# MLP up-projections in a two-layer fp32 transformer: high and low activations side by side, streamed as one run of 512 columns

## The chip, the core and the metric

The kernel runs on one core of a Trainium2 chip. The metric is the device time of one execution in microseconds (us). Of the kernel before, three runs took 1045.91, 1046.89 and 1048.28 us, so the median is 1046.89 us.

## The reference, cut to what matters

Two blocks of a transformer are computed in fp32 for 256 tokens and a model width of 1024. The first block holds two mixing layers; the second holds two layers, each with a mixer, a cross attention and an MLP. Only the MLP is touched:

```
def sq_relu_mlp(h, w_in, w_out):
    return jnp.square(jax.nn.relu(h @ w_in)) @ w_out
```

`h` is 256 x 1024 (normalised tokens), `w_in` 1024 x 4096, `w_out` 4096 x 1024. It runs twice, once in each layer of the second block.

## The kernel before, in words

**Three products for one.** TensorE multiplies operands of the type fp32r, which holds fewer bits than fp32. So every fp32 operand is split into a high part (rounded to fp32r) and a low part (the rest), and a product is made of three matmuls into the same accumulator: high x high, high x low, low x high. The helper `three` (lines 471 to 477) issues them. In a matmul the first operand is the stationary one (128x128, loaded by a weight load of its own, LDWEIGHTS), the second one streams past it, one column after another. In the up-projections the weights are stationary and the activations stream: the names `w_hi`, `w_lo` are the weights' parts, `xT_hi`, `xT_lo` those of the transposed activations, each 128 x 8 chunks x 256 tokens. In the down-projections the activations `hT_hi`, `hT_lo` are stationary, and 512 columns of weights stream.

**Weights.** They arrive in units of 1 MB (2048 columns on 128 partitions) in five slots. SP issues the load of unit u when unit u - 5 has been used by TensorE (the semaphore `units_used`). ScalarE (ACT) then casts the unit's two halves to `w_hi` (line 1233), VectorE (DVE) subtracts to get `w_lo` (line 1715), and TensorE takes a unit when both are there (`lo_ready`).

**The MLP.** Its 4096 hidden features are worked off in 8 blocks of 512. A block needs two units for the up-projection (`up`, each covers 4 of the 8 chunks of the model width) and two for the down-projection (`down`). TensorE's order is written out by hand: first halves of up 0 and up 1, second halves of both, down 0, then for block 2 to 7 `up(blk)` followed by `down(blk - 1)`, and at the end down 7. The down-projections accumulate in banks 0 to 3 over all blocks. The up-projections use two pairs of banks by turns, 4 and 5 for even blocks, 6 and 7 for odd ones: one bank holds two groups of 128 features, 256 token columns each.

**From bank to next operand.** For each block and each of its two banks (pieces p of 128x512), ACT computes the relu out of the bank into `arena` (line 1628) and raises `relu_ready`; DVE squares it (line 2236, `h_ready`); ACT casts the square to `hT_hi` (line 1631, `hhi_ready`); DVE subtracts to get `hT_lo` (line 2239, `hT_ready`). `up(blk)` waits until both relus of block blk - 2 are done, `down(blk)` until both pieces of `hT_lo` are there. In ACT's and DVE's own queues, the work of a block (`step`) stands behind the casts and subtractions of the units up to those of the next up-projection (`splits(u + 6)`), and ahead of the two after them.

The instructions of one `up_half` before (one unit, 48 matmuls) come from these lines:

```
for f in range(4):
    o = banks[A_ + f // 2][:, (f % 2) * S:(f % 2 + 1) * S]
    for c in range(4):
        a = [flat(w, u)[:, c * BLK + f * P:c * BLK + (f + 1) * P] for w in (w_hi, w_lo)]
        ins = three(o, a, [v[:, 4 * n + c, :] for v in X], u, ...)
```

Of the kernel before, what the change touches and what calls it, by code (L numbers as in the profile page):

```python
# [21 lines left out]
ALU = mybir.AluOpType  # L22
# [3 lines left out]
F32R = mybir.dt.float32r  # L26
I32 = mybir.dt.int32

P = 128
D = 1024  # L30
S = 256
T = S // P
KC = D // P
# [10 lines left out]
DFF = 4 * D  # L44
BLK = 512
NBLK = DFF // BLK
MLA_QL, MLA_KVL, NOPE, ROPE, MLA_V = 384, 256, 128, 64, 128
LAM_INIT = 0.8 - 0.6 * math.exp(-0.3)
TWO_PI_HI = 6.28125
# [137 lines left out]
def build(nc, A, out):  # L187
    names, units = weight_units(A)
# [6 lines left out]
    with ExitStack() as ctx:  # L195
        def sb(name, shape, dt=F32):
            return ctx.enter_context(nc.sbuf_tensor(name, shape, dt))

        def sem(name):
            return ctx.enter_context(nc.semaphore(name))  # L200

        w_hi = sb("w_hi", [P, SLOTS, UNIT], F32R)
        raw_at = (nc.sbuf_base + 31) // 32 * 32
        raw = sb("raw", [P, SLOTS, UNIT])
        w_lo = nc.alloc_sbuf_tensor_at("w_lo", [P, SLOTS, UNIT], F32R, offset=raw_at)
        xT_hi = sb("xT_hi", [P, KC, S], F32R)
        xT_lo = sb("xT_lo", [P, KC, S], F32R)
        hT_hi = sb("hT_hi", [P, KC, S], F32R)
        hT_lo = sb("hT_lo", [P, KC, S], F32R)
        x = sb("x", [P, T, D])  # L210
# [24 lines left out]
        banks = [ctx.enter_context(nc.psum_tensor(f"bank{b}", [P, PANEL], F32)) for b in range(8)]  # L235
# [13 lines left out]
        units_used = sem("units_used")  # L249
        written = [sem(f"written{b}") for b in range(8)]  # L250
# [18 lines left out]
        fox_gate, fox_log, fox_sums, fox_ready = sem("fox_gate"), sem("fox_log"), sem("fox_sums"), sem("fox_ready")  # L269
        sb_log, sb_w, angle_ready, sine_ready, lam_sum, lam_exp, gains_ready = (sem(n) for n in ("sb_log", "sb_w", "angle_ready", "sine_ready", "lam_sum", "lam_exp", "gains_ready"))  # L270
        relu_ready, h_ready, hhi_ready, hT_ready = (sem(n) for n in ("relu_ready", "h_ready", "hhi_ready", "hT_ready"))
        setup_ready, out_ready, out_done = sem("setup_ready"), sem("out_ready"), sem("out_done")
        gained_ready, final_rstd, out_right_ready = sem("gained_ready"), sem("final_rstd"), sem("out_right_ready")

# [125 lines left out]
        mlp_base = {}  # L400
        released = {}

        def flat(buf, u):
            return buf[:, u % SLOTS, :]
# [34 lines left out]
        def _(pe):  # L439
            uses = [0] * 8  # L440
            freed = [None] * 8
# [489 lines left out]
            for c in range(5):  # L931
                o = banks[4][:, 0:S] if c < 3 else banks[4][:, S:2 * S]
# [86 lines left out]
            def mlp(i):  # L1019
# [2 lines left out]
                hb = [hT_blocks(v) for v in H]  # L1022

                base = {}
                relu0, hT0 = 2 * NBLK * i, 2 * NBLK * i

                def up_half(odd, n, u):

                    A_ = 4 + 2 * odd
                    take(u)  # L1030
# [4 lines that stand above are left out]
                            ins = three(o, a, [v[:, 4 * n + c, :] for v in X], u, n == 0 and f % 2 == 0 and c == 0, n == 1 and c == 3)  # L1035
                        if n == 1 and f == 1:
                            ins.then_inc(written[A_], 1)
                    ins.then_inc(units_used, 1)

                def up(odd, u, blk):  # L1040
                    pe.wait_ge(relu_ready, relu0 + 2 * (blk - 2) + 2)
                    for n in range(2):
                        up_half(odd, n, u + n)

                def down(odd, u, blk, first, last):

# [55 lines left out]
                down(0, u0 + 4, 0, True, False)  # L1102
                for blk in range(2, NBLK):
                    u = u0 + 6 + 4 * (blk - 2)
                    up(blk % 2, u, blk)
                    down(1 - blk % 2, u + 2, blk - 1, False, False)
                for b in (4, 6):
                    uses[b] += NBLK // 2
                for b in (4, 5, 6, 7):
                    freed[b] = [(relu_ready, relu0 + 2 * NBLK)]  # L1110
# [112 lines left out]
        def _(act):  # L1223
# [389 lines left out]
            def mlp(i):  # L1613
                x_turned(("p", i), U[("xo", i, 1), 0], U["mlp", i])
                u0 = names["mlp", i]
                h0 = 2 * NBLK * i

                def step(blk, u):

                    odd = blk % 2  # L1620
                    splits(u + 6 if blk else u + 5)
                    for p in range(2):
                        b = 4 + 2 * odd + p
                        if p == 0:
                            act.wait_ge(written[b], mlp_base[i][b] + blk // 2 + 1)
                        else:
                            act.wait_ge(units_used, max(u + 2, u0 + 3))
                        nc.scalar.activation(pan(4, p), banks[b][:, :], ACT.Relu).then_inc(relu_ready, 1)
                    for p in range(2):
                        act.wait_ge(h_ready, h0 + 2 * blk + p + 1)  # L1630
                        nc.scalar.copy(hb[:, 2 * odd + p, :], pan(5, p)).then_inc(hhi_ready, 1)

                used(u0 - 1)
                step(0, u0)
                step(1, u0 + 2)
                splits(u0 + 10)
                for blk in range(2, NBLK):
# [67 lines left out]
        def _(dve):  # L1705
# [518 lines left out]

            def mlp(i):
                x_turned(("p", i), ("xo", i), U[("xo", i, 1), 0], U["mlp", i])
                u0, h0 = names["mlp", i], 2 * NBLK * i

                def step(blk, u):
                    odd = blk % 2  # L2230
                    splits(u + 6 if blk else u + 5)
                    for p in range(2):
                        dve.wait_ge(relu_ready, h0 + 2 * blk + p + 1)
                        if p == 0 and (blk > 0 or i > 0):
                            dve.wait_ge(hT_ready, h0 + 2 * blk)
                        V.tensor_tensor(pan(5, p), pan(4, p), pan(4, p), ALU.mult).then_inc(h_ready, 1)
                    for p in range(2):
                        dve.wait_ge(hhi_ready, h0 + 2 * blk + p + 1)
                        V.tensor_tensor(hb[1][:, 2 * odd + p, :], pan(5, p), hb[0][:, 2 * odd + p, :].bitcast(F32),
                                        ALU.subtract).then_inc(hT_ready, 1)  # L2240

                used(u0 - 1)
                step(0, u0)
                step(1, u0 + 2)
                splits(u0 + 10)
                for blk in range(2, NBLK):
                    u = u0 + 6 + 4 * (blk - 2)
                    step(blk, u)
                    splits(u + 8)
# [207 lines left out]
```

## Time and profile before

| what | value |
|---|---|
| median of three runs | 1046.89 us |
| the profiled execution's own time | 1048.91 us |
| its span in the profile | 1047.1 us |
| PE busy, share of the span | 999.7 us, 95% |
| DVE / ACT busy | 629.9 us / 547.5 us |
| TensorE clock granted, mean over the span | 0.977 |
| first MLP, down 0 to the end of up 7 | 524.18 to 658.70 us |
| second MLP, the same stretch | 883.82 to 1018.34 us |

The times in the profile are of one execution: its span is 1047.1 us, and 1.81 us lie around it. A matmul's row in the timeline shows a start and a duration; matmuls are pipelined, so a row lasts longer than the distance to the next one. What one matmul costs a busy TensorE is therefore the distance from start to start, or the length of a stretch divided by its count.

### The profile page before, as it was taken

What the parts mean: (1) busy time and instruction counts of PE and PEld (TensorE: products, weight loads), DVE (VectorE), ACT (ScalarE), POOL (GpSimd) and SP (SyncE); (2) the same over time, 40 slices, a digit from 0 to 9 for tenths busy, and PEclk for the clock granted to TensorE, in tenths of its full rate; (3) what the DMA queues carried; (4) which work ended last, traced back from release to release, by engine and by line L of the source; (5) the groups of instructions that cost most, each with busy time, mean ns of one, the idle gap of its engine ahead of it and who ended that gap; (6) DMA issues with size and microseconds to landing.
All of it is one profiled execution on the core that took longest, in us unless ns stands there. A gap on an engine that the chain in (4) does not pass through costs nothing.

```text
span 1047.1 us, 15752 instructions
## 1 busy us (share of the span) xinstructions
PE 999.7 (95%) x6172; PEld 885.2 (85%) x6172; DVE 629.9 (60%) x1216; ACT 547.5 (52%) x1029; POOL 36.1 (3%) x83
## 2 busy tenths in 40 slices
PE   8999999998899979997999999999999899999997
PEld 7878788886787979895999999899988779999995
DVE  5877554676664476645765554557873658554554
ACT  6586553656474445534654444455663556444452
POOL 4021000001020000000000000000000000000000
PEclk9999989999899989999999999999999989999999
DMA  9975304454232434342555555656435425655651
GB/s 287 242 166 123 102 23 158 161 173 149 81 112 61 110 97 147 121 145 82 177 177 186 200 184 180 240 161 179 144 121 173 150 72 170 200 175 189 199 184 41
DMA packets 114166, 158.14 MB, mean 151 GB/s; under 512 B 13782, under 2 KB 55084, under 8 KB 114092
## 3 DMA queue, kind: packets, MB, share of 16 engines
q1 hardware_dynamic: 113656, 156.56, 48.3%
q8 instruction: 50, 0.82, 0.3%
q10 hardware_dynamic: 436, 0.56, 0.2%
q14 instruction: 24, 0.20, 0.1%
HBM read 156.06 MB, written 1.05 MB: 150 GB/s over the span
## 4 chain that ended last, share of the span: by engine, by line
PE 87%; DVE 7%; ACT 3%; issue 2%; DMA 0%; SPq 0%; DVEq 0%; ACTq 0%
PE bank L475 25%; PE bank L476 25%; PE bank L477 25%; DVE w_lo L1715 2%; PE bank L613 2%; PE bank L638 2%; PE bank L529 2%; PE bank L627 2%; PE bank L607 1%; ACT pb L1397 1%; ACT w_hi L1233 1%; PE bank L592 1%; PE bank L647 0%; DMA raw<-in_w_in_ab 0%; DVE arena L1925 0%
## 5 line engine op out<-in xcount | busy, mean ns | idle before, releaser
L1715 DVE TENSOR_TENSOR w_lo<-raw,w_hi 128x1024 fp32r<-128x1024 f32 (+2 forms) x292 | 335.9, 1196 | 189.6 <-ACT w_hi L1233 189.4
L1233 ACT CAST w_hi<-raw 128x1024 fp32r<-128x1024 f32 (+2 forms) x292 | 283.1, 1026 | 145.6 <-DMA raw<-in_mlp_w_in 76.0
L475 PE MATMUL bank<-xT_hi,w_hi 128*128 128x256 f32 x784 | 223.5, 285 | 2.7 <-DVE xT_lo L1772 1.8
L477 PE MATMUL bank<-xT_hi,w_lo 128*128 128x256 f32 x784 | 221.8, 283 | 0.0
L476 PE MATMUL bank<-xT_lo,w_hi 128*128 128x256 f32 x784 | 221.8, 283 | 0.0
L475 PE MATMUL bank<-w_hi,xT_hi 128*128 128x512 f32 (+1 forms) x432 | 162.7, 377 | 6.9 <-issue 3.2
L477 PE MATMUL bank<-w_hi,xT_lo 128*128 128x512 f32 (+1 forms) x432 | 158.7, 367 | 0.0
L476 PE MATMUL bank<-w_lo,xT_hi 128*128 128x512 f32 (+1 forms) x432 | 158.5, 367 | 0.0
L475 PEld LDWEIGHTS bank<-xT_hi,w_hi 128*128 128x128 f32 x784 | 150.3, 192 | 4.4 <-issue 2.6
L476 PEld LDWEIGHTS bank<-xT_lo,w_hi 128*128 128x128 f32 x784 | 150.3, 192 | 0.6
L477 PEld LDWEIGHTS bank<-xT_hi,w_lo 128*128 128x128 f32 x784 | 150.3, 192 | 0.0
L475 PE MATMUL bank<-w_hi,hT_hi 128*128 128x512 f32 (+2 forms) x384 | 143.8, 375 | 0.5 <-DVE hT_lo L1770 0.5
L476 PE MATMUL bank<-w_lo,hT_hi 128*128 128x512 f32 (+2 forms) x384 | 143.1, 373 | 0.0
L477 PE MATMUL bank<-w_hi,hT_lo 128*128 128x512 f32 (+2 forms) x384 | 142.7, 372 | 0.0
L475 PEld LDWEIGHTS bank<-w_hi,xT_hi 128*128 128x128 f32 x432 | 83.6, 194 | 20.9 <-issue 8.8
L477 PEld LDWEIGHTS bank<-w_hi,xT_lo 128*128 128x128 f32 x432 | 83.1, 192 | 13.4
L476 PEld LDWEIGHTS bank<-w_lo,xT_hi 128*128 128x128 f32 x432 | 83.6, 193 | 11.8
L475 PEld LDWEIGHTS bank<-w_hi,hT_hi 128*128 128x128 f32 x384 | 72.9, 190 | 13.3 <-DVE hT_lo L1770 0.9
L477 PEld LDWEIGHTS bank<-w_hi,hT_lo 128*128 128x128 f32 x384 | 72.6, 189 | 12.8
L476 PEld LDWEIGHTS bank<-w_lo,hT_hi 128*128 128x128 f32 x384 | 72.7, 189 | 11.9
L1772 DVE SCALAR_TENSOR_TENSOR xT_lo<-bank,gains,xT_hi 128x256 fp32r<-128x256 f32 x76 | 31.9, 478 | 37.8 <-ACT xT_hi L1278 37.8
L1291 ACT ACTIVATE xn<-x 128x512 f32<-128x512 f32 x32 | 20.1, 629 | 55.0 <-DVE x L1841 49.5
(242 smaller groups left out, 1107.7 us busy)
## 6 DMA issues: line engine op xcount, KB each, us to landing
raw<-in_mlp_w_in SPq DMA_DIRECT2D x32, 1024.0 KB, 5.3
raw<-in_mlp_w_out SPq DMA_DIRECT2D x32, 1024.0 KB, 5.1
raw<-in_w_in_ab SPq DMA_DIRECT2D x13, 1024.0 KB, 10.2
raw<-in_w_in_cd SPq DMA_DIRECT2D x13, 1024.0 KB, 5.2
raw<-in_xa_w_kv SPq DMA_DIRECT2D x8, 1024.0 KB, 5.2
raw<-in_sb_w_qkv SPq DMA_DIRECT2D x16, 512.0 KB, 5.1
raw<-in_w_out_ab SPq DMA_DIRECT2D x4, 1024.0 KB, 5.0
raw<-in_w_out_cd SPq DMA_DIRECT2D x4, 1024.0 KB, 5.1
```

The lines of the kernel that those rows point to most:

```text
L475: pe.matmul(o, wh, ih, start=start, stop=False, skip_group_check=True)
L476: pe.matmul(o, wh, il, start=False, stop=False, skip_group_check=True)
L477: return pe.matmul(o, wl, ih, start=False, stop=stop, skip_group_check=True)
L529: ins = pe.transpose(o, src(t, c), ident[:, :])
L592: ins = pe.transpose(o, arena[:, panel, t * w + c * P:t * w + (c + 1) * P], ident[:, :])
L613: ins = pe.matmul(banks[b][:, a:z], q(t * P, (t + 1) * P), kk(0, keys), start=n == 0, stop=n == len(k["parts"]) - 1)
L627: ins = pe.transpose(banks[6][:, n * P:(n + 1) * P], src[:, a:a + P], ident[:, :])
L638: ins = pe.matmul(banks[7][:, t * vd:(t + 1) * vd], k["pt"][:, n * P:(n + 1) * P], k["v"](kt), start=m == 0, stop=m == len(mine) - 1)
L1233: nc.scalar.copy(w_hi[:, u % SLOTS, a], raw[:, u % SLOTS, a]).then_inc(hi_ready, 1)
L1291: ins = nc.scalar.activation(xn[:, t, a], x[:, t, a], ACT.Square, accum_out=(guess if half else ssq)[:, c:c + 1])
L1715: V.tensor_tensor(w_lo[:, u % SLOTS, a], raw[:, u % SLOTS, a], w_hi[:, u % SLOTS, a].bitcast(F32), ALU.subtract).then_inc(lo_ready, 1)
L1772: ins = V.scalar_tensor_tensor(out=o, in0=ps, scalar=g, in1=hi.bitcast(F32), op0=ALU.mult, op1=ALU.subtract)
```

## The change

The two parts of the activations become one tensor `xT` with the high and the low part of a chunk side by side (256 + 256 columns). In the up-projections of blocks 2 to 7 the high weights of one chunk and one feature group are loaded once and stream all 512 columns, into a whole bank: the first 256 columns collect high x high, the last 256 high x low. The low weights then stream the 256 high columns into the first half. So a bank holds one group of 128 features, with its sum in two halves, and a block takes all four banks 4 to 7. The up-projection waits for each bank separately, for the block just before it.

Emptying a bank is another sequence: ACT copies the second half into `arena`, DVE adds the first half to it (this frees the bank, `relu_ready`), and DVE computes relu and square in one instruction over two groups. Blocks 0 and 1 stay as they were.

```diff
+RELUS = 4 + 4 * (NBLK - 2)
-        xT_hi = sb("xT_hi", [P, KC, S], F32R)
-        xT_lo = sb("xT_lo", [P, KC, S], F32R)
+        xT = sb("xT", [P, KC, 2, S], F32R)
+        xT_hi, xT_lo = xT[:, :, 0, :], xT[:, :, 1, :]
...
-                def up(odd, u, blk):
-                    pe.wait_ge(relu_ready, relu0 + 2 * (blk - 2) + 2)
+                def up(u, blk):
+
                     for n in range(2):
-                        up_half(odd, n, u + n)
+                        take(u + n)
+                        for f in range(4):
+                            b = 4 + f
+                            if n == 0:
+                                pe.wait_ge(relu_ready, relu0 + 4 * (blk - 2) + f + 1)
+                            for c in range(4):
+                                k = 4 * n + c
+                                wh, wl = (flat(w, u + n)[:, c * BLK + f * P:c * BLK + (f + 1) * P] for w in (w_hi, w_lo))
+                                pe.matmul(banks[b][:, :], wh, xT[:, k].rearrange("p a s -> p (a s)"), start=k == 0, stop=False, skip_group_check=True)
+                                ins = pe.matmul(banks[b][:, 0:S], wl, xT_hi[:, k, :], start=False, stop=k == KC - 1, skip_group_check=True)
+                            if n == 1 and f < 3:
+                                ins.then_inc(written[b], 1)
+                        ins.then_inc(units_used, 1)
```

On ScalarE, in the step of a block:

```diff
-                    for p in range(2):
+                    for p in range(2 if blk < 2 else 0):
...
+                    for f in range(4 if blk >= 2 else 0):
+                        if f < 3:
+                            act.wait_ge(written[4 + f], mlp_base[i][4 + f] + blk - f % 2)
+                        else:
+                            act.wait_ge(units_used, u + 2)
+                        nc.scalar.copy(pan(4, f // 2)[:, f % 2 * S:(f % 2 + 1) * S], banks[4 + f][:, S:2 * S]).then_inc(second_ready, 1)
```

On VectorE, in the step of a block from block 2 on, in place of the square:

```diff
+                        for f in (2 * p, 2 * p + 1):
+                            o = pan(4, p)[:, f % 2 * S:(f % 2 + 1) * S]
+                            dve.wait_ge(second_ready, second0 + 4 * (blk - 2) + f + 1)
+                            V.tensor_tensor(o, banks[4 + f][:, 0:S], o, ALU.add).then_inc(relu_ready, 1)
+                            own.last = (relu_ready, relu0 + 4 * (blk - 1) + f + 1)
+                        own.settle()
+                        V.scalar_tensor_tensor(out=pan(5, p), in0=pan(4, p), scalar=0.0, in1=pan(4, p), op0=ALU.max, op1=ALU.mult).then_inc(h_ready, 1)
```

TensorE, the start of up 2 in the first MLP, before:

```order
L475 MATMUL bank<-xT_hi,w_hi 128x256 [waits lo_ready,relu_ready]
L476 MATMUL bank<-xT_lo,w_hi 128x256
L477 MATMUL bank<-xT_hi,w_lo 128x256
L475 MATMUL bank<-xT_hi,w_hi 128x256
L476 MATMUL bank<-xT_lo,w_hi 128x256
L477 MATMUL bank<-xT_hi,w_lo 128x256
```

The same place now (`xT` is the new tensor; the first eight rows fill bank 4, the ninth row begins bank 5):

```order
L1053 MATMUL bank<-xT,w_hi 128x512 [waits relu_ready,lo_ready]
L1054 MATMUL bank<-xT,w_lo 128x256
L1053 MATMUL bank<-xT,w_hi 128x512
L1054 MATMUL bank<-xT,w_lo 128x256
L1053 MATMUL bank<-xT,w_hi 128x512
L1054 MATMUL bank<-xT,w_lo 128x256
L1053 MATMUL bank<-xT,w_hi 128x512
L1054 MATMUL bank<-xT,w_lo 128x256
L1053 MATMUL bank<-xT,w_hi 128x512 [waits relu_ready]
```

Three matmuls of 256 columns have become one of 512 and one of 256, and a block waits for its banks in four places instead of one.

VectorE, the step of block 2 in the first MLP, before (`arena` holds the relu and its square; L1715 splits weights):

```order
L1715 TENSOR_TENSOR w_lo<-raw,w_hi 128x1024 [waits hi_ready] x8
L2236 TENSOR_TENSOR arena<-arena 128x512 [waits hT_ready,relu_ready]
L2236 TENSOR_TENSOR arena<-arena 128x512 [waits relu_ready]
L2239 TENSOR_TENSOR hT_lo<-arena,hT_hi 128x512 [waits hhi_ready] x2
L1715 TENSOR_TENSOR w_lo<-raw,w_hi 128x1024 [waits hi_ready] x8
```

And now:

```order
L1735 TENSOR_TENSOR w_lo<-raw,w_hi 128x1024 [waits hi_ready] x8
L2262 TENSOR_TENSOR arena<-bank,arena 128x256 [waits second_ready,hT_ready]
L2262 TENSOR_TENSOR arena<-bank,arena 128x256 [waits second_ready]
L2265 SCALAR_TENSOR_TENSOR arena<-arena 128x512 [waits relu_ready]
L2262 TENSOR_TENSOR arena<-bank,arena 128x256 [waits second_ready] x2
L2265 SCALAR_TENSOR_TENSOR arena<-arena 128x512 [waits relu_ready]
L2269 TENSOR_TENSOR hT_lo<-arena,hT_hi 128x512 [waits hhi_ready] x2
L1735 TENSOR_TENSOR w_lo<-raw,w_hi 128x1024 [waits hi_ready] x8
```

Four additions out of the banks have come in, and they are what a later up-projection waits for; the weight subtractions stand around the step as before.

## Rows read from the trace of the kernel before

**Rows 1.** The page: the chain that ended last, by engine.

```profile
PE 87%; DVE 7%; ACT 3%; issue 2%; DMA 0%; SPq 0%; DVEq 0%; ACTq 0%
```

**Rows 2.** Busy time by stretch; last columns: granted clock, DMA share, GB/s.

```profile
core 0: us, PE busy (x) PEld busy (x) DVE busy (x) ACT busy (x) POOL busy (x), PEclk, DMA share, GB/s
535.08:546.60 11.52, 11.52 (x98) 11.51 (x97) 4.72 (x4) 4.13 (x5) 0.00 (x0) 1.00 0.58 182
546.60:557.50 10.90, 10.90 (x50) 9.01 (x49) 7.23 (x8) 5.97 (x8) 0.00 (x0) 1.00 0.58 194
524.18:658.70 134.52, 134.52 (x867) 123.17 (x866) 73.62 (x74) 61.49 (x74) 0.00 (x0) 1.00 0.59 192
883.82:1018.34 134.52, 134.52 (x867) 123.17 (x866) 73.61 (x74) 61.69 (x74) 0.00 (x0) 1.00 0.58 192
840.00:850.00 10.00, 8.65 (x26) 6.36 (x25) 4.91 (x7) 5.99 (x9) 0.00 (x0) 0.55 0.00 1
```

**Rows 3.** PE timeline at down 1 to up 3: start, duration, instruction.

```profile
557.28 0.39 PE L477 MATMUL bank<-w_hi,hT_lo 128*128 128x512 f32 x1
557.50 0.28 PE L475 MATMUL bank<-xT_hi,w_hi 128*128 128x256 f32 x1
557.62 0.28 PE L476 MATMUL bank<-xT_lo,w_hi 128*128 128x256 f32 x1
```

**Rows 4.** PE timeline where 128 columns follow 256, in the latent attention.

```profile
382.57 0.28 PE L477 MATMUL bank<-hT_hi,w_lo 128*128 128x256 f32 x1
382.69 0.22 PE L475 MATMUL bank<-w_hi,hT_hi 128*128 128x128 f32 x1
382.75 0.28 PE L476 MATMUL bank<-w_lo,hT_hi 128*128 128x128 f32 x1
382.87 0.27 PE L477 MATMUL bank<-w_hi,hT_lo 128*128 128x128 f32 x1
```

**Rows 5.** PE's weight loads in up 2 (timeline).

```profile
543.00 0.19 PEld L476 LDWEIGHTS bank<-xT_lo,w_hi 128*128 128x128 f32 x1
543.12 0.19 PEld L477 LDWEIGHTS bank<-xT_hi,w_lo 128*128 128x128 f32 x1
```

**Rows 6.** ACT timeline, end of up 2 and end of up 7.

```profile
546.37 2.00 ACT L1233 CAST w_hi<-raw 128x1024 fp32r<-128x1024 f32 x2 [3.60 <-DMA raw<-in_mlp_w_in]
548.27 1.07 ACT L1628 ACTIVATE arena<-bank 128x512 f32<-128x512 f32 x2
550.45 1.23 ACT L1631 CAST hT_hi<-arena 128x512 fp32r<-128x512 f32 x2 [1.10 <-DVE arena L2236]
...
660.22 1.07 ACT L1628 ACTIVATE arena<-bank 128x512 f32<-128x512 f32 x2
```

**Rows 7.** DVE timeline, the same two places.

```profile
547.45 2.36 DVE L1715 TENSOR_TENSOR w_lo<-raw,w_hi 128x1024 fp32r<-128x1024 f32 x2 [3.25 <-ACT w_hi L1233]
551.11 1.30 DVE L2239 TENSOR_TENSOR hT_lo<-arena,hT_hi 128x512 fp32r<-128x512 f32 x2
...
659.40 2.36 DVE L1715 TENSOR_TENSOR w_lo<-raw,w_hi 128x1024 fp32r<-128x1024 f32 x2 [3.43 <-ACT w_hi L1233]
```

**Rows 8.** Groups by line and shape: busy us, mean ns, idle before.

```profile
L1337 ACT COPY row<-bank 128x256 f32<-128x256 f32 x5 | 1.8, 370 | 5.5 <-PE bank L559 5.5
L2195 DVE TENSOR_TENSOR arena<-bank,arena 128x256 f32<-128x256 f32 x8 | 3.4, 423 | 6.9 <-ACT arena L1585 6.9
L2239 DVE TENSOR_TENSOR hT_lo<-arena,hT_hi 128x512 fp32r<-128x512 f32 x32 | 20.9, 690 | 1.4
L2310 DVE SCALAR_TENSOR_TENSOR x<-bank,ssq,x 128x512 f32<-128x512 f32 x4 | 3.0, 750 | 9.9 <-PE bank L477 9.9
```

**Rows 9.** Waits (us in total, times, longest) and DMA issues (KB, us to landing).

```profile
ACT w_hi L1233 <- DMA raw<-in_mlp_w_in: 76.0, 20, 4.9
...
raw<-in_mlp_w_in SPq DMA_DIRECT2D x32, 1024.0 KB, 5.3
...
raw<-in_w_in_ab SPq DMA_DIRECT2D x13, 1024.0 KB, 10.2
```

More of the change, by code:

```diff
@@ L271, in build @@
         relu_ready, h_ready, hhi_ready, hT_ready = (sem(n) for n in ("relu_ready", "h_ready", "hhi_ready", "hT_ready"))
+        second_ready = sem("second_ready")
         setup_ready, out_ready, out_done = sem("setup_ready"), sem("out_ready"), sem("out_done")
@@ L1024, in mlp @@
                 base = {}
-                relu0, hT0 = 2 * NBLK * i, 2 * NBLK * i
+                relu0, hT0 = RELUS * i, 2 * NBLK * i
                 def up_half(odd, n, u):
@@ L1104, in mlp @@
                     u = u0 + 6 + 4 * (blk - 2)
-                    up(blk % 2, u, blk)
+                    up(u, blk)
                     down(1 - blk % 2, u + 2, blk - 1, False, False)
-                for b in (4, 6):
-                    uses[b] += NBLK // 2
+                for b, n in ((4, NBLK - 1), (5, NBLK - 2), (6, NBLK - 1)):
+                    uses[b] += n
                 for b in (4, 5, 6, 7):
-                    freed[b] = [(relu_ready, relu0 + 2 * NBLK)]
+                    freed[b] = [(relu_ready, relu0 + RELUS)]
                 if i == 0:
@@ L1621, in step @@
                     splits(u + 6 if blk else u + 5)
-                    for p in range(2):
+                    for p in range(2 if blk < 2 else 0):
                         b = 4 + 2 * odd + p
                         if p == 0:
-                            act.wait_ge(written[b], mlp_base[i][b] + blk // 2 + 1)
+                            act.wait_ge(written[b], mlp_base[i][b] + 1)
                         else:
@@ L2226, in mlp @@
                 x_turned(("p", i), ("xo", i), U[("xo", i, 1), 0], U["mlp", i])
-                u0, h0 = names["mlp", i], 2 * NBLK * i
+                u0, h0, relu0, second0 = names["mlp", i], 2 * NBLK * i, RELUS * i, 4 * (NBLK - 2) * i
                 def step(blk, u):
@@ L2232, in step @@
                     for p in range(2):
-                        dve.wait_ge(relu_ready, h0 + 2 * blk + p + 1)
                         if p == 0 and (blk > 0 or i > 0):
                             dve.wait_ge(hT_ready, h0 + 2 * blk)
-                        V.tensor_tensor(pan(5, p), pan(4, p), pan(4, p), ALU.mult).then_inc(h_ready, 1)
+                        if blk < 2:
+                            dve.wait_ge(relu_ready, relu0 + 2 * blk + p + 1)
+                            V.tensor_tensor(pan(5, p), pan(4, p), pan(4, p), ALU.mult).then_inc(h_ready, 1)
+                            continue
+                        for f in (2 * p, 2 * p + 1):
[5 more added lines that the diff above has]
+                        V.scalar_tensor_tensor(out=pan(5, p), in0=pan(4, p), scalar=0.0, in1=pan(4, p), op0=ALU.max, op1=ALU.mult).then_inc(h_ready, 1)
+                        own.last = (h_ready, h0 + 2 * blk + p + 1)
                     for p in range(2):
```

## The prediction, made before the changed kernel ran

> **What bounds the kernel now.** The page first: the chain that ended last lies 87% on TensorE [rows 1], so a cheaper stretch of matmuls shortens the whole, provided nothing else is late in it. Next the busy time by stretch: up 2 (535.08 to 546.60) lasts 11.52 us and down 1 behind it 10.90 us, and PE is busy for the whole of both. From down 0 to the end of up 7 it is busy for all of 134.52 us, in the first MLP as in the second: six rounds of 22.42 us without one gap, at a granted clock of 1.00 [rows 2]. In these rounds nothing but TensorE's own pace counts.
>
> The pace is read from start to start. An up-projection has 4 groups x 8 chunks x 3 = 96 matmuls of 256 columns, and 11.52 / 96 = 0.120 us each. A down-projection has 2 x 2 x 4 x 3 = 48 of 512 columns, and 10.90 / 48 = 0.227 us each [rows 2]. Both stand in the timeline: 557.28 to 557.50 for 512 columns, 557.50 to 557.62 for 256 [rows 3].
>
> **What a merged matmul saves.** Two streams of 256 columns cost 0.240 us, one of 512 costs 0.227. The columns are the same, so what goes is a fixed part of 0.013 us per matmul. A third width says the same: a 128-column matmul at 382.69 is followed by the next one after 0.06 us, at 382.75 [rows 4]. A line of 0.0533 us per 128 columns plus 0.0133 gives 0.067, 0.120 and 0.227 for the three widths. The second 128-column matmul then takes 0.12 us, not 0.067: there the weight load sets the pace, about 0.11 to 0.12 us [rows 4]. Under 256 columns (0.120 us) a load is just covered, under 512 amply. In the new order high weights are loaded under a 256-column stream, as two loads in three are today, and low weights under one of 512.
>
> Per feature group and chunk: before 3 x 0.120 = 0.360 us, after 0.227 + 0.120 = 0.347 us. A block has 32 such pairs, so an up-projection falls from 11.52 to 11.11 us, by 0.413. Two MLPs have 6 changed blocks each: 12 x 0.413 = **4.96 us**. Blocks 0 and 1 keep their form.
>
> No row shows a 512-column matmul into a bank in turn with a 256-column one into its half. From the nearest rows: the second costs at least half of a 512-column one, 0.1135 us, which makes the pair 0.3405 and the gain 7.5 us. At worst it gives the fixed part back, pair 0.360, gain 0. The change of width at 557.50 shows 0.22 and then 0.12 us with nothing between [rows 3], and 12 matmuls in a row into one bank run at 0.227 in the down-projections; so I take 0.347.
>
> Two rules of the Trainium skill are weighed here. The trace first: the weight loads of up 2 start 0.12 us apart and are shown with 0.19 us each [rows 5], and all 96 pairs of load and matmul pass in 11.52 us. The page "TensorE: Matmul & The Clock Gate", section "Measured speedup vs the span model", says that a weight load overlaps matmuls in flight only when it goes to other rows of the array; these loads take all rows. By that rule each of the 384 removed loads would save its whole time, which at the 0.11 us of rows 4 would be 42 us, and the kernel would take about 1005 us. The trace disagrees: load and stream in series need over 0.2 us, and 0.120 is measured. The same page, section "Wait — 56ns, not 53.3ns?", has a fixed cost of about 2.5 ns per matmul at full clock; by it the edit would save 384 x 0.0025 = 1.0 us. The trace shows 13 ns; the measurement decides.
>
> **Waits.** SP's loads keep their order. Before, an up-projection waited for relus of two blocks earlier, long done. Now up(blk + 1) waits for additions of block blk, with only down(blk - 1), 10.90 us, between. Take up 2, which ends at 546.60. ACT is in its weight casts until about 548.3 [rows 6], then come 4 copies of 256 columns out of a bank, 0.370 us each [rows 8]: the first is done at 548.7, the last at 549.8. DVE subtracts weights until 549.81 [rows 7]. Then two additions at 0.423 us [rows 8], a relu and square, two additions, a relu and square. The 512-column scalar_tensor_tensor is not in the trace with both inputs in SBUF; between 0.690 (a tensor_tensor there) and 0.750 (one out of a bank) [rows 8] I take 0.72. The first addition is done at 550.2, the fourth at 552.2 (549.81 + 4 x 0.423 + 0.72), the last square at 553.0 with some 0.05 for the waits of DVE on itself. Up 3 needs the first bank at 546.60 + 10.90 = 557.50, the fourth 3 x 4 pairs or 4.2 us later. So the slack is 7.3 us for the first bank and 9.5 for the fourth: the wait costs nothing.
>
> What queues behind it: ACT's casts of hT (0.61 each, [rows 6]) and DVE's two subtractions (0.65 each, [rows 7]) end at about 554.3 instead of 552.4, since the second cast waits for 553.0. Then come the next weights. They are for down 2, at 569.0, and start about 2 us later, with 11 us to spare. The tightest place is the end of an MLP, where down 7 needs hT only one down-projection after up 7: up 7 ends at 658.70, DVE is free at 659.40 + 2.36 = 661.76 [rows 7], plus 4.5 is 666.3, against 669.60. Slack 3.3 us, cost nothing. DVE has the room: it is busy 4.72 + 7.23 = 11.95 of 22.42 us per round [rows 2]; 4 x 0.423 and 2 x 0.03 more make 13.7. ACT has 4 x 0.370 for 2 x 0.535, 0.4 us more.
>
> **The sum.** 1048.91 us for the profiled execution (span 1047.1 + 1.81 around it) less 4.96 is 1043.95. That execution is 2.02 us above the median of the runs, so on the median the forecast is 1046.89 - 4.96 = **1041.9 us**.
>
> **Rivals.**
> 1. The merged form gives the fixed part back (a high-weight load not quite covered under 256 columns, or a price for changing width each time). For it: the 0.19 us shown for a load [rows 5]; loads at 0.11 to 0.12 [rows 4] have almost no margin under 0.120. Against: today's up-projection has every load under 256 columns and makes 0.120. Gain 0: 1046.9 us.
> 2. Slower: the banks come back too late. Place: the wait of an up-projection for the additions of the block before it. ACT's copies stand behind the casts of the next up's second unit, whose load SP issues when half of the up-projection is over, 5.6 us before its end, and which lands in 5.3 us [rows 9]. It decides once the first addition ends more than 7.3 us later than worked out, so a landing of 12.6 us; each microsecond beyond costs up to 12 us over both MLPs, and from 0.41 beyond it the kernel is slower than before. At 1 us beyond: 1046.89 - 4.96 + 12 = 1053.9 us. For it: the first loads of the program took 10.2 us [rows 9]. Against: the longest wait for such a unit is 4.9 us where 3.6 is usual [rows 6, 9].
> 3. The 256-column matmul behind a 512-column one costs only half of the latter: gain 7.5, 1039.4 us.
> 4. The rounds save as worked out, but the low-clock stretch between the MLPs (0.55 in 840 to 850, [rows 2]) falls otherwise since all there comes 2.5 us sooner. Ten microseconds at 0.55 cost some 4 us, and a third of that may go or come: 1040.6 to 1043.3 us. This lies inside the forecast's own range.
> 5. The change does not do what it says: the order shows 384 fewer matmuls with 12 x 32 of 512 columns, so I leave it out.
>
> **How the numbers follow.** Forecast with its clock scatter 0.88, rival 1 0.05, rival 2 0.02, rival 3 0.05. About 0.2% (2.1 us) is what a measurement of this kernel can tell from no change. Faster by more than that: forecast, rival 3 and a little less for the half-way cases, 0.92. Within: rival 1 and half of its gain, 0.06. Slower: 0.02. The range takes the forecast with 1.3 us of clock and runs either side, and a part of the way to rivals 3 and 1, since the unseen price is bounded by them: 1040.0 to 1044.2 us.
>
> **What would show it.** In the changed profile the stretch from the start of down 0 to the end of up 7 is 132.04 us in each MLP (134.52 - 6 x 0.413), PE busy all of it; up 3 lasts 11.1 us and starts right behind down 1; the starts of high and low matmuls alternate at 0.23 and 0.12 us. An idle time of PE before the 512-column line that ends with the addition on DVE shows rival 2. A pair of 0.36 us without idle shows rival 1, one of 0.34 rival 3. Nothing changes in the stretches outside the MLPs but the low-clock one. The prediction is wrong if the rounds take over 22.2 us or another stretch moves by more than 1.5 us.

## The result, and the profile after

Seven runs of the changed kernel took 1039.56 to 1043.94 us, median 1040.11; seven of the kernel before had a median of 1046.89. The medians differ by 6.78 us. The estimate of the ratio from all runs is 0.9942, with a 95% interval of 0.9928 to 0.9957, which is about 6.1 us (4.5 to 7.5). Repeated in another session, beside experiments, it was 1041.52 against 1047.74 us, ratio 0.9942 (0.992 to 0.9964).

The forecast was 1041.9 us in a range of 1040.0 to 1044.2. The number holds. The account behind it holds in half: the matmuls gave back 2.3 us and not 4.96, and a low-clock stretch that did not come gave 3.4 us.

The chain that ended last in the profile after is TensorE's again, with a little less of it [rows 1]:

```profile
PE 83%; DVE 7%; ACT 4%; issue 3%; DMA 2%; SPq 1%; DVEq 0%; ACTq 0%
```

Busy time by stretch in the profile after: up 2, down 1, the two MLP stretches from down 0 to the end of up 7, what lies between them, and 840 to 850, the stretch that [rows 2] has with a clock of 0.55 (the same work now comes 2.46 us sooner in it). The columns are those of [rows 2].

```profile
533.76:545.05 11.29, 11.29 (x65) 9.80 (x64) 4.72 (x4) 4.10 (x5) 0.00 (x0) 1.00 0.57 186
545.05:556.00 10.95, 10.95 (x51) 9.02 (x50) 8.73 (x12) 6.19 (x11) 0.00 (x0) 1.00 0.62 192
522.86:656.22 133.36, 133.36 (x675) 112.87 (x673) 81.14 (x94) 61.66 (x84) 0.00 (x0) 1.00 0.60 193
877.96:1011.33 133.37, 133.37 (x675) 112.88 (x674) 81.14 (x94) 61.84 (x84) 0.00 (x0) 1.00 0.58 193
656.22:877.96 221.74, 213.73 (x1522) 199.38 (x1521) 143.70 (x238) 123.41 (x222) 0.00 (x0) 1.00 0.50 155
840.00:850.00 10.00, 9.21 (x39) 7.36 (x40) 6.42 (x8) 5.79 (x10) 0.00 (x0) 1.00 0.11 20
```

The stretch between the MLPs in the profile before:

```profile
658.70:883.82 225.12, 217.54 (x1523) 202.25 (x1522) 142.36 (x234) 123.26 (x220) 0.00 (x0) 0.98 0.48 153
```

So the two profiled executions differ by 1048.91 - 1041.92 = 6.99 us, and it can be laid out: 1.32 ahead of the first MLP stretch (524.18 against 522.86), 1.16 in the first MLP, 225.12 - 221.74 = 3.38 between, 1.15 in the second, nothing behind it. The 1.32 is no effect of the change. Over all 14 profiles of this study that part, in which no kernel issues other work, ended between 521.5 and 525.4 us. Without it 2.31 + 3.38 = 5.7 us is left, which lies inside the interval of 4.5 to 7.5 us.

The timeline of TensorE at the start of up 3 in the profile after (start, duration, instruction):

```profile
555.77 0.39 PE L479 MATMUL bank<-w_hi,hT_lo 128*128 128x512 f32 x1
556.00 0.39 PE L1053 MATMUL bank<-xT,w_hi 128*128 128x512 f32 x1
556.22 0.28 PE L1054 MATMUL bank<-xT,w_lo 128*128 128x256 f32 x1
556.34 0.40 PE L1053 MATMUL bank<-xT,w_hi 128*128 128x512 f32 x1
556.57 0.28 PE L1054 MATMUL bank<-xT,w_lo 128*128 128x256 f32 x1
556.69 0.40 PE L1053 MATMUL bank<-xT,w_hi 128*128 128x512 f32 x1
556.93 0.28 PE L1054 MATMUL bank<-xT,w_lo 128*128 128x256 f32 x1
```

The first one of 512 columns takes 0.22 us, the later ones 0.23 to 0.24. In the trace's starts they repeat 232, 241 and 235 ns, and the narrow ones 114, 118 and 120: 236 + 117 = 353 ns a pair, not 347.

The emptying of the banks of block 2 (four copies on ACT, four additions and two relu-and-squares on DVE), first ACT, then DVE, in the profile after (up 2 ends at 545.05):

```profile
546.79 1.18 ACT L1648 COPY arena<-bank 128x256 f32<-128x256 f32 x4
549.76 0.62 ACT L1651 CAST hT_hi<-arena 128x512 fp32r<-128x512 f32 x1 [1.78 <-DVE arena L2265]
551.15 0.62 ACT L1651 CAST hT_hi<-arena 128x512 fp32r<-128x512 f32 x1 [0.77 <-DVE arena L2265]
```

```profile
548.25 0.75 DVE L2262 TENSOR_TENSOR arena<-bank,arena 128x256 f32<-128x256 f32 x2
549.03 0.69 DVE L2265 SCALAR_TENSOR_TENSOR arena<-arena 128x512 f32<-128x512 f32 x1
549.64 0.75 DVE L2262 TENSOR_TENSOR arena<-bank,arena 128x256 f32<-128x256 f32 x2
550.42 0.69 DVE L2265 SCALAR_TENSOR_TENSOR arena<-arena 128x512 f32<-128x512 f32 x1
551.03 1.46 DVE L2269 TENSOR_TENSOR hT_lo<-arena,hT_hi 128x512 fp32r<-128x512 f32 x2
```

The fourth addition ends at 549.64 + 0.75 = 550.39, 5.3 us behind the end of up 2 (forecast 5.6), and hT is ready after 7.4 us (forecast 7.7). Up 3 starts right behind down 1, at 556.00.

### The profile page after: what moved, and what is told of

The parts are those of the page before. It is cut to its first block, busy times and chain, and to the rows that moved or that the text cites. A ratio compares the mean times of both kernels' runs of the same rounds, so it can differ in the third digit from the quotient of the medians.

```text
span 1040.1 us, 15056 instructions
## 1 busy us (share of the span) xinstructions
PE 989.8 (95%) x5788; PEld 857.7 (82%) x5788; DVE 647.7 (62%) x1264; ACT 548.1 (53%) x1053; POOL 35.5 (3%) x83
## 4 chain that ended last, share of the span: by engine, by line
PE 83%; DVE 7%; ACT 4%; issue 3%; DMA 2%; SPq 1%; DVEq 0%; ACTq 0%
PE bank L477 20%; PE bank L478 20%; PE bank L479 20%; PE bank L1053 9%; PE bank L1054 4%; DVE w_lo L1735 3%; PE bank L615 2%; PE bank L640 2%; PE bank L531 2%; PE bank L629 1%; DMA raw<-in_w_in_ab 1%; PE bank L609 1%; ACT pb L1411 1%; DMA x<-in_x 1%; ACT w_hi L1247 1%
## 5 line engine op out<-in xcount | busy, mean ns | idle before, releaser
L477 PE MATMUL bank<-w_hi,xT 128*128 128x512 f32 (+1 forms) x432 | 162.6, 376 | 6.9 <-issue 3.2
L478 PE MATMUL bank<-w_lo,xT 128*128 128x512 f32 (+1 forms) x432 | 158.9, 368 | 0.0
L479 PE MATMUL bank<-w_hi,xT 128*128 128x512 f32 (+1 forms) x432 | 158.6, 367 | 0.0
L1053 PE MATMUL bank<-xT,w_hi 128*128 128x512 f32 x384 | 136.0, 398 | 0.0
L477 PE MATMUL bank<-xT,w_hi 128*128 128x256 f32 x400 | 114.9, 287 | 2.7 <-DVE xT L1792 1.8
L479 PE MATMUL bank<-xT,w_lo 128*128 128x256 f32 x400 | 113.1, 283 | 0.0
L478 PE MATMUL bank<-xT,w_hi 128*128 128x256 f32 x400 | 113.1, 283 | 0.0
L1054 PE MATMUL bank<-xT,w_lo 128*128 128x256 f32 x384 | 107.8, 281 | 0.0
L477 PEld LDWEIGHTS bank<-w_hi,xT 128*128 128x128 f32 x432 | 83.3, 193 | 21.1 <-issue 8.8
L479 PEld LDWEIGHTS bank<-w_hi,xT 128*128 128x128 f32 x432 | 83.1, 192 | 13.6
L478 PEld LDWEIGHTS bank<-w_lo,xT 128*128 128x128 f32 x432 | 83.2, 192 | 12.0
L1053 PEld LDWEIGHTS bank<-xT,w_hi 128*128 128x128 f32 x384 | 72.2, 188 | 17.8
L477 PEld LDWEIGHTS bank<-xT,w_hi 128*128 128x128 f32 x400 | 76.6, 191 | 4.0 <-issue 2.7
L478 PEld LDWEIGHTS bank<-xT,w_hi 128*128 128x128 f32 x400 | 76.7, 192 | 0.2
```

What stands on the lines that cost most here:

```text
L477: pe.matmul(o, wh, ih, start=start, stop=False, skip_group_check=True)
L478: pe.matmul(o, wh, il, start=False, stop=False, skip_group_check=True)
L479: return pe.matmul(o, wl, ih, start=False, stop=stop, skip_group_check=True)
L1053: pe.matmul(banks[b][:, :], wh, xT[:, k].rearrange("p a s -> p (a s)"), start=k == 0, stop=False, skip_group_check=True)
L1054: ins = pe.matmul(banks[b][:, 0:S], wl, xT_hi[:, k, :], start=False, stop=k == KC - 1, skip_group_check=True)
```

## The experiments

Each ran in the number of executions named, with runs of the kernel before taken in the same session. "MLP stretch" is always from down 0 to the end of up 7, "between" from there to down 0 of the second MLP. The count of executions stands in brackets behind a time. "Wide" is a matmul of 512 columns, "narrow" one of 256.

**1. The layout alone.**

```diff
-        xT_hi = sb("xT_hi", [P, KC, S], F32R)
-        xT_lo = sb("xT_lo", [P, KC, S], F32R)
+        xT = sb("xT", [P, KC, 2, S], F32R)
+        xT_hi, xT_lo = xT[:, :, 0, :], xT[:, :, 1, :]
```

> The kernel before with the two parts of the activations in one tensor, high and low side by side; nothing else is changed. Theory A (the 3.8 to 4.5 us that the changed kernel saves outside the two MLP stretches are low-clock stretches that fell elsewhere because everything came sooner): the layout does nothing, 1046.9 us, within 0.2% of before, MLP stretches 134.5 us each. Rival B (the layout itself helps, in the reads or writes of xT in all stages): 1042.5 to 1043 us, with the saving outside the MLPs.

Measured: 1047.75 us (12) against 1047.72 (29), ratio 1.0 (0.9985 to 1.0015). MLP stretches 134.52, between 225.14. The layout does nothing by itself.

**2. Banks and emptying as changed, matmuls as before.**

```diff
-                                pe.matmul(banks[b][:, :], wh, xT[:, k].rearrange("p a s -> p (a s)"), start=k == 0, stop=False, skip_group_check=True)
+                                pe.matmul(banks[b][:, 0:S], wh, xT_hi[:, k, :], start=k == 0, stop=False, skip_group_check=True)
+                                pe.matmul(banks[b][:, S:2 * S], wh, xT_lo[:, k, :], start=False, stop=False, skip_group_check=True)
```

> The changed kernel, its four banks per block and its way of emptying them kept, but with three streams of 256 columns in place of 512 and 256. If the way of emptying and the waits cost nothing: an up-projection lasts 11.52 us, the stretch from down 0 to the end of up 7 lasts 134.5 us, and the kernel takes 1046.9 us if the pace of TensorE is all that made the changed kernel faster. Rival B (layout) says 1042.5 to 1043. If the small additions to the down-projections (10.95 for 10.90 us) come from the extra copies and additions, they stay: 134.8 us.

Measured: 1046.51 us (12) against 1047.72, ratio 0.9993 (0.9979 to 1.0007). Between the MLPs it has 225.11 us, with the low clock of before. Up 2, down 1 and the MLP stretch in its profile:

```profile
532.39:543.90 11.51, 11.51 (x98) 11.51 (x96) 4.72 (x4) 3.85 (x5) 0.00 (x0) 1.00 0.56 182
543.90:554.81 10.91, 10.91 (x51) 9.01 (x50) 8.73 (x12) 6.20 (x11) 0.00 (x0) 1.00 0.58 194
521.48:656.00 134.52, 134.52 (x867) 123.14 (x865) 81.16 (x94) 61.86 (x84) 0.00 (x0) 1.00 0.59 192
```

134.52 us, to the hundredth that of before, with the new copies, additions and waits all in (DVE 81.16 for 73.62 us): they cost TensorE nothing. Down 1 is at 10.91 again, so the 0.05 us by which it became longer in the changed kernel (10.95 for 10.90) go with the wide matmuls.

**3. Four wide streams, then four narrow ones.**

```diff
                             for c in range(4):
                                 k = 4 * n + c
-                                wh, wl = (flat(w, u + n)[:, c * BLK + f * P:c * BLK + (f + 1) * P] for w in (w_hi, w_lo))
+                                wh = flat(w_hi, u + n)[:, c * BLK + f * P:c * BLK + (f + 1) * P]
                                 pe.matmul(banks[b][:, :], wh, xT[:, k].rearrange("p a s -> p (a s)"), start=k == 0, stop=False, skip_group_check=True)
+                            for c in range(4):
+                                k = 4 * n + c
+                                wl = flat(w_lo, u + n)[:, c * BLK + f * P:c * BLK + (f + 1) * P]
                                 ins = pe.matmul(banks[b][:, 0:S], wl, xT_hi[:, k, :], start=False, stop=k == KC - 1, skip_group_check=True)
```

> The changed kernel with the four streams of 512 columns of a group first and its four streams of 256 behind them, instead of by turns. Measured by turns: 0.236 and 0.117 us, a pair of 0.353 where 0.347 was forecast. Theory C (each change of width costs some 3 ns): 8 changes per group become 2, a pair takes 0.348 us, an up-projection 11.15 us, the kernel 12 x 0.14 = 1.7 us less than the changed one. Rival D (a 512-column stream costs more after any load of high weights, or for another reason of its own): no gain, 11.29 us. Rival E: the 0.006 us belong to the pair of loads, and 256-column streams behind each other give 0.120, 512-column ones 0.236: 11.4 us.

Measured: 1040.95 us (6) against 1047.72, ratio 0.9935 (0.9915 to 0.9955). Up 11.20 us, MLP stretches 132.74, between 221.74. Theory C had 11.15: right in direction, but it forecast 0.14 us less where 0.09 came. A wide stream is slow not once per change of width but several times in a row behind narrow ones.

**4. One more wide matmul per up-projection.**

```diff
+                                if k == 0 and f == 0:
+                                    pe.matmul(banks[b][:, :], wh, xT[:, k].rearrange("p a s -> p (a s)"), start=True, stop=False, skip_group_check=True)
```

> The changed kernel with one more matmul of 512 columns per up-projection (the first one of a block issued twice), which makes a round as long as before, 22.4 us. Work added: 12 x 0.23 = 2.7 us. Theory A1 (where the low-clock stretches fall depends on the time since the start, so before's positions bring before's low clock back): 1046.9 us, mean clock 0.977 as before. Rival A2 (they fall by chance, or depend on something else that the change has altered): the changed kernel's time plus 2.7, 1042.8 to 1043.5 us, clock about 0.985.

Measured: 1046.98 us (12) against 1047.72, ratio 0.9992 (0.9977 to 1.0008), mean clock 0.982. The time is A1's, the clock lies between the two. In its profile the MLP stretches are 134.72 and 134.73 and the part between 223.25, with no low clock at 838 but 0.89 in 755 to 770. So it is neither theory as written: the work between loses time to a low clock again, 1.5 us instead of 3.4, in another place.

**5. The changed kernel again.** 

> The changed kernel once more, beside the others. Measured so far: 1040.11 us, 1.16 us less in each MLP stretch and 3.4 us less between them, where before has a low-clock stretch at 838.9 us that the changed kernel lacks. If that belongs to the kernel: 1040 to 1041.5 us against 1047.7 of before, clock about 0.984, and 221.7 us between the MLP stretches again. If it was chance, on repetition the kernel is 2.3 to 3.5 us faster than before, not 6.

Measured: 1041.52 us (9), ratio 0.9942 (0.992 to 0.9964), clock 0.983 against 0.979 of before, 221.77 us between. The missing low-clock stretch belongs to the kernel.

**6 and 7. The wide form in one MLP alone.** In experiment 7 the condition is `i == 1`.

```diff
+                                if i == 0:
                                     pe.matmul(banks[b][:, :], wh, xT[:, k].rearrange("p a s -> p (a s)"), start=k == 0, stop=False, skip_group_check=True)
+                                else:
+                                    pe.matmul(banks[b][:, 0:S], wh, xT_hi[:, k, :], start=k == 0, stop=False, skip_group_check=True)
+                                    pe.matmul(banks[b][:, S:2 * S], wh, xT_lo[:, k, :], start=False, stop=False, skip_group_check=True)
```

> The changed kernel with the 512-column form in the first MLP alone; the second one has three streams of 256 columns in the new banks (which cost the same as before, 134.52 us a stretch). Theory F (the time saved between the MLPs comes from all work behind the first MLP running 1.2 us sooner, so that the low-clock stretch behind the second cross attention does not come): 1.16 us less in the first MLP, 3.4 less between, so about 4.5 us less than before, 1043 us. Rival G (the wide form raises the clock wherever it stands, or the gain is chance): half of the changed kernel's gain, 1044.5, and no difference to the run with the wide form in the second MLP alone.

> The mirror image: 512-column form in the second MLP alone. Theory F: 1.16 us less in the second MLP and nothing before it, the stretch between the MLPs 225.1 us with its low clock at about 838: 1046.5 us. Rival G: 1044.5 us, as the other half.

Measured: wide first 1043.66 us (9), ratio 0.9953 (0.9933 to 0.9973); wide second 1045.76 us (12), ratio 0.9979 (0.9963 to 0.9994); before 1047.74 for both. The first MLP stretch, the part between and the second one, wide first:

```profile
524.10:657.46 133.36, 133.36 (x674) 112.85 (x673) 81.16 (x94) 61.79 (x84) 0.00 (x0) 1.00 0.60 193
657.46:879.24 221.78, 213.72 (x1522) 199.37 (x1521) 143.75 (x238) 123.19 (x222) 0.00 (x0) 1.00 0.50 155
879.24:1013.76 134.52, 134.52 (x866) 123.16 (x865) 81.19 (x94) 61.73 (x84) 0.00 (x0) 1.00 0.59 191
```

Wide second:

```profile
524.05:658.57 134.52, 134.52 (x866) 123.15 (x865) 81.16 (x94) 61.81 (x84) 0.00 (x0) 1.00 0.57 192
658.57:883.70 225.13, 217.55 (x1522) 202.27 (x1521) 143.94 (x238) 123.16 (x222) 0.00 (x0) 0.98 0.49 153
883.70:1017.06 133.36, 133.36 (x674) 112.86 (x673) 81.16 (x94) 61.76 (x84) 0.00 (x0) 1.00 0.59 193
```

The third column from the right is the granted clock. Each wide MLP saves its 1.16 us; the 3.35 us between go with the first alone. The ratio of the second would allow G too, the profile does not.

**8. The kernel before with 2.28 us of work more.** The 19 matmuls write into a bank that the next one begins anew, so their results are not used.

```diff
+                            if i == 0 and u == u0 + 6 and f == 0 and c == 0:
+                                for _ in range(19):
+                                    pe.matmul(o, a[0], xT_hi[:, 0, :], start=True, stop=False, skip_group_check=True)
```

> The kernel before with 19 idle matmuls of 256 columns at the start of up 2 of the first MLP, which add 19 x 0.12 = 2.28 us of work there. Theory F (it is the position in time of the work between the MLPs that decides whether the low-clock stretch at 838 comes, and another shift than the changed kernel's can avoid it too): it may vanish, and then the kernel with more work is 3.4 - 2.3 = 1.1 us faster than before, 1046.6 us. Rival G and the plain sum: 1047.7 + 2.3 = 1050.0 us, with the low-clock stretch at 841.

Measured: 1046.5 us (11) against 1047.74, ratio 0.9985 (0.9969 to 1.0001). The plain sum would be a ratio of 1.0022, which lies outside. In its profile, in the same order:

```profile
522.75:659.55 136.80, 136.80 (x885) 125.43 (x884) 73.61 (x74) 61.53 (x74) 0.00 (x0) 1.00 0.57 188
659.55:881.32 221.77, 213.70 (x1523) 199.39 (x1522) 142.19 (x234) 123.09 (x220) 0.00 (x0) 1.00 0.50 155
881.32:1015.84 134.52, 134.52 (x867) 123.16 (x866) 73.60 (x74) 61.53 (x74) 0.00 (x0) 1.00 0.58 192
```

The first stretch is longer by 2.28 us, the part between shorter by 3.35: more work, and no slower beyond the interval. Nothing of the changed kernel is in this one, so its gain between the MLPs is a matter of when that work comes, not of what it is.

**9. Sixteen wide streams, then sixteen narrow ones.** The loops of experiment 3 with the second `for c` moved behind all four `f`.

```diff
+                        for f in range(4):
+                            b = 4 + f
                             for c in range(4):
                                 k = 4 * n + c
+                                wl = flat(w_lo, u + n)[:, c * BLK + f * P:c * BLK + (f + 1) * P]
                                 ins = pe.matmul(banks[b][:, 0:S], wl, xT_hi[:, k, :], start=False, stop=k == KC - 1, skip_group_check=True)
```

> The changed kernel with all 16 streams of 512 columns of a unit first and its 16 of 256 behind them. Seen so far: by turns a pair costs 0.353 us, in fours 0.350 (an up-projection 11.20 us), and in the timeline of the fours the first 512-column streams behind a stretch of 256-column ones are 5 to 10 ns slower, those behind many others of 512 are not. If that is the whole of it, one such start per unit costs some 0.04 us: an up-projection of 11.107 + 0.04 to 0.09, 11.15 to 11.20 us, MLP stretches 132.4 to 132.7 us. If the width change does not matter and fours were only lucky: 11.29. The kernel: 1040 to 1041 us.

Measured: 1039.62 us (6) against 1045.59, ratio 0.9927 (0.9904 to 0.995). Up 2, down 1, and the three parts:

```profile
533.81:544.92 11.11, 11.11 (x66) 9.84 (x65) 4.72 (x4) 3.83 (x5) 0.00 (x0) 1.00 0.60 189
544.92:555.82 10.90, 10.90 (x51) 9.01 (x49) 8.73 (x12) 6.34 (x11) 0.00 (x0) 1.00 0.57 192
522.90:654.98 132.08, 132.08 (x675) 113.10 (x674) 81.13 (x94) 61.64 (x84) 0.00 (x0) 1.00 0.60 194
654.98:878.10 223.12, 215.10 (x1523) 200.81 (x1522) 143.81 (x238) 123.49 (x222) 0.00 (x0) 0.99 0.49 154
```

11.11 us is what the prediction had for 32 pairs of 227 and 120 ns; this experiment's own expectation, 11.15 to 11.20 us, was missed. In the trace's starts the wide streams behind the 512-column ones of down run at 227 at once; those behind sixteen narrow ones need 233, 236, 229, 232 and 231 ns, then 227. The other way round time comes back: the first narrow stream behind wide ones takes 113 or 114 ns instead of 120. By turns, every wide stream follows a narrow one, and none gets back to 227. But between the MLPs a low clock is back, at another place (0.89 in 755 to 770).

**10. The narrow products into the other half of the bank.**

```diff
-                                ins = pe.matmul(banks[b][:, 0:S], wl, xT_hi[:, k, :], start=False, stop=k == KC - 1, skip_group_check=True)
+                                ins = pe.matmul(banks[b][:, S:2 * S], wl, xT_hi[:, k, :], start=False, stop=k == KC - 1, skip_group_check=True)
```

> The changed kernel with the low-weight products added to the second half of the bank instead of the first; the sum of both halves is the same. If a pair costs 0.353 instead of 0.347 because a 512-column stream begins in the columns that the one before has just written: 0.347, an up-projection of 11.11 us. If it is the change of width alone: 11.29 us again. One look, for the up-projections alone.

One execution, 1042.08 us; up 11.29 us. Into which half of the bank the narrow stream writes plays no part.

**11. The fours again.** 

> The fours once more, beside the whole unit. MLP stretches 132.74 us each again, 221.7 between them, 1040.3 to 1041 us; if the whole-unit order brings 11.15 us, this one is 0.6 us behind it.

Measured: 1039.9 us (6), ratio 0.9938 (0.9916 to 0.996); 132.74, 221.75, 132.74. The stages repeat; the medians of two sessions (1040.95, 1039.9) are further apart than the versions.

**12. Fours in the first MLP, sixteens in the second.**

```diff
+                        group = 4 if i else 1
+                        for f0 in range(0, 4, group):
+                            for low in range(2):
+                                for f in range(f0, f0 + group):
...
```

> Fours (four streams of 512 columns, then four of 256) in the first MLP, the whole-unit order (16 and 16) in the second. The whole-unit order in both has 132.08 us in each MLP stretch but 223.12 between them, with a low-clock stretch at 762.6; the fours have 132.74 in each and 221.75 between. Theory F (the shift that the first MLP gives the rest decides about the low clock between): 132.74 + 221.75 + 132.08, so 0.7 us less than either, about 1039 us, no low clock at 762. Rival G (the low-clock stretch at 762 comes by chance or goes with the whole-unit order): no difference to the whole-unit kernel beyond 0.3 us, or the low clock at 762 again.

Measured: 1040.38 us (6) against 1047.77, ratio 0.9928 (0.9908 to 0.9949). The three parts:

```profile
525.35:658.09 132.74, 132.74 (x675) 112.93 (x673) 81.16 (x94) 61.61 (x84) 0.00 (x0) 1.00 0.58 194
658.09:879.81 221.72, 213.67 (x1522) 199.40 (x1521) 143.75 (x238) 123.33 (x222) 0.00 (x0) 1.00 0.50 155
879.81:1011.89 132.08, 132.08 (x674) 113.11 (x673) 81.17 (x94) 61.70 (x84) 0.00 (x0) 1.00 0.59 195
```

The parts are those that theory F named, 486.54 us in all, against 487.28 for experiment 9 and 488.47 for the changed kernel. In the whole time the 0.7 us cannot be seen: the ratios 0.9927 and 0.9928 are equal. Experiments 9 and 12 both have a ratio below the changed kernel's 0.9942, with intervals that overlap; by the stages they are 1.2 and 1.9 us faster.

## Why the prediction was right in its number and half right in its reasons

**The pair of matmuls: the term that was mis-sized.** 0.347 us was forecast for 0.227 + 0.120, measured is 0.353. Of 4.96 us, 2.31 came (133.36 and 133.37 for 134.52). Up 2 became shorter by 0.23 us instead of 0.413, and down 1 behind it, which was to stay as it was, longer by 0.05. The prediction had bounded the unseen sequence by 0.3405 and 0.360 and taken the sum of its parts, on the evidence of one change of width, at 557.50 [rows 3]. That was a change from wide to narrow. The cost is on the other side: the first five or so wide streams behind narrow ones are 2 to 9 ns slower than 227, and by turns all are, by 5 to 14. Experiments 3 and 9 show it: it fades with the grouping (11.29, 11.20, 11.11 us). Experiment 10 shows that the half of the bank written does not matter. The fixed part of 13 ns per matmul was right: with sixteens the 11.11 us forecast is met.

The trace of before had this change too, and the prediction did not use it. Here is the start of down 1 behind up 2, TensorE's timeline in the kernel before:

```profile
546.48 0.28 PE L477 MATMUL bank<-xT_hi,w_lo 128*128 128x256 f32 x1
546.60 0.40 PE L475 MATMUL bank<-w_hi,hT_hi 128*128 128x512 f32 x1
546.83 0.40 PE L476 MATMUL bank<-w_lo,hT_hi 128*128 128x512 f32 x1
547.07 0.39 PE L477 MATMUL bank<-w_hi,hT_lo 128*128 128x512 f32 x1
547.29 0.40 PE L475 MATMUL bank<-w_hi,hT_hi 128*128 128x512 f32 x1
547.53 0.39 PE L476 MATMUL bank<-w_lo,hT_hi 128*128 128x512 f32 x1
```

In the trace's starts the first five take 234, 235, 229, 232 and 231 ns, and the first narrow one at 557.50 takes 113. These rows would have shown that both changes of width have a price of their own. They would not have given 353 ns: 234 + 113 is 347 again. That TensorE does not settle between two changes was seen only in the changed kernel.

Why wide streams are slow behind narrow ones stays open. A weight load that is not quite covered (rival 1) does not fit. The loads at the same place in the kernel before:

```profile
546.48 0.19 PEld L475 LDWEIGHTS bank<-w_hi,hT_hi 128*128 128x128 f32 x1
546.60 0.19 PEld L476 LDWEIGHTS bank<-w_lo,hT_hi 128*128 128x128 f32 x1
546.83 0.19 PEld L477 LDWEIGHTS bank<-w_hi,hT_lo 128*128 128x128 f32 x1
```

The load for the matmul at 546.83 starts at 546.60, so it has 0.23 us, twice the time that loads have among the narrow streams; and yet 546.60 to 546.83 is one of the slow steps.

The rule of the Trainium skill that a load of all rows does not overlap matmuls in flight ("TensorE: Matmul & The Clock Gate") would have given about 1005 us; the runs stay with the trace of before, 0.120 us for load and stream. The rule stands in the page's section "The mechanism", and not in the one that the prediction names; that section also says that a load into the background weight buffer is pulled ahead of matmuls in flight. Which buffer a load takes is shown by no run here. The 2.5 ns of the same page's "Wait — 56ns, not 53.3ns?" would have given 1.0 us for both MLPs; experiment 9 saves 4.88, that is 12.7 ns for each of 384 matmuls.

**The waits: right.** The new bank order costs nothing (experiment 2), and the times worked out for copies, additions and hT are met within 0.3 us. Rival 2 never came near: the first bank is free some 7 us before it is needed. DVE's 13.45 us per round (4.72 + 8.73) against 13.7 forecast.

**The clock between the MLPs: named, but under-sized and taken for scatter.** Rival 4 let it move by 1.3 us either way. It moved by 3.38 us, and on repetition by 3.35 the same way. In both kernels TensorE stands still for 2.59 us in the second cross attention. Here is the matmul behind that pause, before:

```profile
838.34 0.69 PE L647 MATMUL bank<-arena,mem 128*128 128x256 f32 x2 [2.59 <-DVE hT_lo L1770]
```

and after:

```profile
835.88 0.67 PE L649 MATMUL bank<-arena,mem 128*128 128x256 f32 x2 [2.59 <-DVE hT_lo L1790]
```

Before, the granted clock falls to the lower level (1.2 GHz) just behind it, and the work of the next ten microseconds runs at it ([rows 2], 840 to 850, 0.55). The first matmuls of the output projection, of 512 columns, start 0.43 us apart, about twice the 0.227 of the full clock:

```profile
848.16 0.63 PE L475 MATMUL bank<-w_hi,hT_hi 128*128 128x512 f32 x1
848.59 0.63 PE L476 MATMUL bank<-w_lo,hT_hi 128*128 128x512 f32 x1
```

After, the clock stays at 1.00. The pause is the same and the work around it too; what differs is when it comes. Experiments 6 and 7 show that only the shift from the first MLP counts, and experiment 8 that added work does it as well as a saving.

"When" is not the time since the start of the profile. In experiment 2 the pause ends sooner than in the changed kernel, and the low clock comes all the same. Its timeline, and its busy time by stretch with a granted clock of 0.66:

```profile
835.65 0.67 PE L649 MATMUL bank<-arena,mem 128*128 128x256 f32 x2 [2.59 <-DVE hT_lo L1791]
835.00:850.00 15.00, 13.00 (x41) 9.98 (x42) 7.79 (x14) 7.88 (x15) 0.00 (x0) 0.66 0.00 0
```

Counted from down 0 of the first MLP the profiles fall apart cleanly. The pause ends 314.2 us behind it in the four with this low clock (before, experiments 1, 2 and 7). In the ten without, it ends 312.4 to 313.1 or 315.9 to 316.5 us behind it.

**By its own tests** the prediction's account fails twice: it would be wrong "if the rounds take over 22.2 us" (they take 22.23) "or another stretch moves by more than 1.5 us" (3.38). Two misses of opposite sign, 2.6 us too much and 3.4 too little, left the sum inside the range. That is luck: nothing in the prediction's working ties the one to the other.

**Left open.** Which shifts avoid the low clock. Against the kernel before, the first MLP was shorter by 1.16 and 1.78 us or longer by 2.28, and no low clock came between the MLPs; at 0 it came at 838, at 0.2 longer and 2.44 shorter in 755 to 770. That is the list, not a rule, and most points rest on one profile each, with medians that agree. That it is the 2.59 us pause which brings the clock down was not tried by removing the pause. In experiments 4 and 9 the low clock begins behind another pause, of 1.77 us, in the second layer's mixer part (at 765.01 and 762.90), which the kernel before has too, at 766.62, without a low clock.

## What to carry to other kernels

Where TensorE has no gap, price an order of matmuls from starts in the trace, and for each kind of neighbour: a narrow stream behind a wide one is not the same as the other way round, and streams of one width belong together. Ask of every saving what it shifts: here a part that the change does not touch gave more (3.4 us) than the edit did (2.3). So measure an edit by its own stretch, which repeats to 0.01 us here, and distrust a match of the total.

## What the runs showed of the hardware

- Adding work can cost nothing: 2.28 us of matmuls more in the kernel before, and the median went from 1047.74 to 1046.5 us (ratio 0.9985, 0.9969 to 1.0001).
- At the full clock a weight load with its matmul costs 0.120 and 0.227 us for 256 and 512 columns among their like; in alternation the two take 0.353 together. The 0.067 us that the prediction's line gives for 128 columns stands in no run: right behind a 256-column stream it is 0.06 once [rows 4], then 0.11 to 0.12.
- The first streams behind a change of width differ: 234, 235, 229, 232 and 231 ns for 512 columns behind 256, and 113 for 256 behind 512 (kernel before, at 546.60 and 557.50).
- Executions of one kernel follow their clock: of 29 runs of before in one session, the fastest had 1043.92 us at a mean granted clock of 0.984, the slowest 1052.09 at 0.974. Over all 29 the correlation of time and clock is -0.86.
